# Pooling branch of a mixer: u computed in turned form, window sums by shifted adds on VectorE instead of band matrix products on TensorE

## What is computed

```python
proj = h @ w_in                      # h: 256 x 1024, w_in: 1024 x 2048
q, k, v, u = proj[..., :512], proj[..., 512:1024], proj[..., 1024:1536], proj[..., 1536:]
a = chunked_attention(q, k, v, ...)  # 8 heads of 64
# pooling, group g with window w in (2, 4, 8, 16):
win_sum = c[:, 1:] - c[:, start]     # trailing sum over at most w frames
outs.append(win_sum / count - uf)    # count = min(t + 1, w)
y = einsum('bsgc,gcd->bsgd', d, pool_w) * pool_scale
out = concatenate([a, y], -1) @ w_out
```

## Time and profile before

| | |
|---|---|
| time of 3 runs, median (lowest to highest) | 713.96 us (713.49 to 714.18) |
| the profiled execution: its own time, its span | 713.59 us, 711.8 us |
| TensorE busy | 701.5 us, 99% of the span |
| VectorE, ScalarE, GpSimd busy | 482.0, 378.8, 59.0 us |
| chain of work that ended last | 98% on TensorE |

### The profile page before, as it was taken

How to read it: one execution, slowest core, us unless ns; L and a number is a source line. 1 busy time by engine, 2 the same in 40 slices (tenths; PEclk the granted TensorE clock), 3 DMA queues, 4 the chain that set the end, 5 groups by cost and what they waited for, 6 DMA issues and landing times.

```text
span 711.8 us, 9748 instructions
## 1 busy us (share of the span) xinstructions
PE 701.5 (99%) x3734; PEld 596.0 (84%) x3734; DVE 482.0 (68%) x730; ACT 378.8 (53%) x517; POOL 59.0 (8%) x36
## 2 busy tenths in 40 slices
PE   8999999999999999999999999999999999999995
PEld 7888888888888688888888888888888888878884
DVE  5696777755476456777776855466763738898756
ACT  6764555444376555754445644477444534675450
POOL 1000000000000400000000000000005172131001
PEclk9999999999999999999999999999999999999999
DMA  8987555555345314655455566436574183443001
GB/s 306 356 329 279 192 206 188 178 186 210 136 181 232 120 52 156 243 197 201 185 177 185 199 215 232 177 126 229 186 253 148 40 316 121 175 161 135 1 1 59
DMA packets 21523, 129.33 MB, mean 182 GB/s; under 512 B 2456, under 2 KB 4400, under 8 KB 7280
## 3 DMA queue, kind: packets, MB, share of 16 engines
q1 hardware_dynamic: 19872, 126.72, 48.8%
q10 hardware_dynamic: 1344, 1.32, 0.6%
q0 software_dynamic: 272, 0.81, 0.3%
HBM read 127.79 MB, written 1.06 MB: 181 GB/s over the span
## 4 chain that ended last, share of the span: by engine, by line
PE 98%; DVE 1%; DMA 1%; issue 0%; ACT 0%; DVEq 0%; POOLq 0%
PE ps L421 23%; PE ps L386 16%; PE ps L388 16%; PE ps L387 16%; PE ps L427 12%; PE ps L406 3%; PE ps L410 2%; PE ps L633 1%; PE ps L564 1%; PE ps L982 1%; PE ps L804 1%; PE ps L440 1%; DMA sm<-in_sm 1%; PE ps L580 1%; PE ps L688 1%; PE ps L690 1%
## 5 line engine op out<-in xcount | busy, mean ns | idle before, releaser
L1495 DVE TENSOR_TENSOR wlo<-raw,whi 128x2048 fp32r<-128x2048 f32 x69 | 159.1, 2314 | 39.0 <-ACT whi L1056 38.8
L1056 ACT ACTIVATE whi<-raw 128x2048 fp32r<-128x2048 f32 x78 | 148.8, 1910 | 44.2 <-PE ps L388 42.0
L421 PE MATMUL ps<-xt,whi 128*128 128x512 f32 x704 | 168.4, 391 | 0.0
L421 PEld LDWEIGHTS ps<-xt,whi 128*128 128x128 f32 x704 | 129.4, 188 | 25.0
L386 PE MATMUL ps<-whi,xt 128*128 128x512 f32 (+1 forms) x304 | 121.8, 401 | 0.1
L388 PE MATMUL ps<-whi,xt 128*128 128x512 f32 (+1 forms) x304 | 117.0, 385 | 0.0
L387 PE MATMUL ps<-wlo,xt 128*128 128x512 f32 (+1 forms) x304 | 116.8, 384 | 0.0
L427 PEld LDWEIGHTS ps<-xt,wlo 128*128 128x128 f32 x704 | 90.3, 191 | 3.4
L427 PE MATMUL ps<-xt,wlo 128*128 128x256 f32 x704 | 91.3, 283 | 0.0
L1448 POOL TENSOR_TENSOR wlo<-raw,whi 128x2048 fp32r<-128x2048 f32 (+1 forms) x9 | 41.0, 4559 | 549.6 <-ACT whi L1056 549.6
L1100 ACT ACTIVATE work<-ps 128x512 f32<-128x512 f32 x44 | 26.2, 598 | 96.1 <-PE ps L421 91.2
(11 more groups left out here) (238 smaller groups left out, 740.2 us busy)
## 6 DMA issues: line engine op xcount, KB each, us to landing
raw<-in_gu SPq DMA_DIRECT2D x41, 1024.0 KB, 4.8
raw<-in_dn SPq DMA_DIRECT2D x22, 1024.0 KB, 4.7
raw<-in_win SPq DMA_DIRECT2D x8, 1024.0 KB, 4.8
raw<-in_fqk SPq DMA_DIRECT2D x8, 1024.0 KB, 4.8
raw<-in_wout SPq DMA_DIRECT2D x4, 1024.0 KB, 5.2
raw<-in_fg SPq DMA_DIRECT2D x4, 1024.0 KB, 4.8
raw<-in_fv SPq DMA_DIRECT2D x4, 1024.0 KB, 4.8
raw<-in_fo SPq DMA_DIRECT2D x4, 1024.0 KB, 4.7
```

Source lines behind the costliest of these rows:

```text
L421: return pe.matmul(ps[:, banks[u], :], wh[:, k * S + u * P:k * S + (u + 1) * P], x, start=k == 0, stop=k == KD - 1)
L1056: act.activation(whi[:, c % RING, 0:n], raw[:, c % RING, 0:n], ACT.Copy).then_inc(hi_ready, 1)
L1495: dve.tensor_tensor(wlo[:, c % RING, 0:n], raw[:, c % RING, 0:n], whi[:, c % RING, 0:n].bitcast(F32), ALU.subtract).then_inc(lo_ready, 1)
```

## The change

TensorE now computes u already turned (channels on the partitions, frames along the row): the weights are stationary, 128 columns at a time, and the 256 frames move. `u_step(step)` has four channel blocks of three products of 256 columns, 12 products in place of 6; two steps make one group, and the groups come in the order of windows 16, 8, 4, 2. The band matrices and the copies to `u_sb` are gone, and with them the 8 band products, their 2 copies to `d_t`, and 1,472 of the 4,096 columns of a parameter transfer.

In their place: `mixer_row` turns the frames' scale factors into a row (2 transposes on TensorE, one copy `row(1, 3, mix_row)` on ScalarE ahead of `hi(C_WIN+5+RING)`). VectorE multiplies each group of u by that row into a padded row `u_pad` (`pool_begin`), forms window sums by doubling (`doubled`: the row plus itself shifted by 1, 2, 4, 8), corrects the first 16 frames (`fewer`) and takes the mean minus the frame into `d_t` (`pool_end`). Every such step waits for the one ahead of it. That is 4 multiplications, 10 doublings, 4 corrections and 4 final steps, put into the head loop behind `probs_out`; the last group's stand ahead of `outputs_lo(0)`. Four small memsets clear the pads earlier. The `pool_w` products wait for all four groups (`pooled`). GpSimd's program is the same as before.

```diff
+            def mixer_row():
+                pe.wait_ge(rstd_ready, 2)
+                for t in range(NT):
+                    m = pe.transpose(ps[:, 3, t * P:(t + 1) * P], rstd[:, t:t + 1].broadcast_to([P, P]), ident)
+                m.then_inc(row_psum, 1)
...
-            def u_step(k):
-                wh, wl = take(C_WIN + 6 + k // HALF)
-                for t in range(NT):
-                    w = slice((k % HALF) * BANK, (k % HALF + 1) * BANK)
-                    m = three(ps[:, 2 + t, :], xth[:, k, t * P:(t + 1) * P], xtl[:, k, t * P:(t + 1) * P], wh[:, w], wl[:, w], k == 0, k == KD - 1)
+            def u_step(step):
+                p, k0 = step // 2, step % 2 * HALF
+                wh, wl = take(C_WIN + 6 + p // 2)
+                if p == 1 and k0 == 0:
+                    pe.wait_ge(row_ready, 2)
+                if p >= 2 and k0 == 0:
+                    pe.wait_ge(u_turned, 4 + p - 1)
+                for k in range(k0, k0 + HALF):
+                    w = slice(k * S + p % 2 * P, k * S + p % 2 * P + P)
+                    m = three(ps[:, 2 + p % 2, 0:S], wh[:, w], wl[:, w], xth[:, k, :], xtl[:, k, :], k == 0, k == KD - 1)
...
+            mixer_row()
             u_step(0)
             scores1(0)
             for h in range(H1):
...
-                    pe.wait_ge(par_landed, 16)
-                    pe.wait_ge(u_ready, 2)
-                    for g in range(4):
-                        o = ps[:, 2 + g // 2, (g % 2) * S:(g % 2) * S + S]
-                        pe.matmul(o, u_sb[:, 0, g * P:(g + 1) * P], band[:, g, 0:S], start=True, stop=False)
-                        m = pe.matmul(o[:, P:S], u_sb[:, 1, g * P:(g + 1) * P], band[:, g, S:S + P], start=False, stop=True)
...
+            pe.wait_ge(par_landed, 16)
+            pe.wait_ge(pooled, 4)
             for g in range(4):
-                pe.wait_ge(d_act if g // 2 else d_dve, 1)
...
+            row(1, 3, mix_row)
             hi(C_WIN + 5 + RING)
...
+            def pool_step(i):
+                i.then_inc(pool_order, 1)
+                n_pool[0] += 1
+                dve.wait_ge(pool_order, n_pool[0])
...
+            def doubled(p, j):
+                src = u_pad[p % 2] if j == 0 else sum_pad[(j - 1) % 2]
+                back = 1 << j
+                pool_step(dve.tensor_tensor(sum_pad[j % 2][:, PAD:PAD + S], src[:, PAD:PAD + S], src[:, PAD - back:PAD + S - back], ALU.add))
...
+            def pool_begin(p):
...
+                dve.tensor_tensor(u[:, PAD:PAD + S], ps[:, 2 + p % 2, 0:S], mix_row, ALU.mult).then_inc(u_turned, 1)
+                dve.wait_ge(u_turned, 4 + p + 1)
+                for j in range((4 - p) // 2):
+                    doubled(p, j)
...
+            def pool_end(p):
+                g = 3 - p
+                for j in range((4 - p) // 2, 4 - p):
+                    doubled(p, j)
+                total = sum_pad[(3 - p) % 2]
+                first = total[:, PAD:2 * PAD]
+                pool_step(dve.tensor_tensor(first, first, fewer[:, g, :], ALU.mult))
+                dve.scalar_tensor_tensor(out=d_t[:, g, :], in0=total[:, PAD:PAD + S], scalar=1.0 / WINDOWS[g], in1=u_pad[p % 2][:, PAD:PAD + S],
+                                         op0=ALU.mult, op1=ALU.subtract).then_inc(pooled, 1)
...
             for h in range(H1):
                 masked(0, h, lambda t: bias1[:, h, P:2 * P] if t == 0 else bias1[:, h, :], 4)
-                if h == H1 - 1:
-                    dve.wait_ge(chunk_used, C_WIN + 8)
-                    dve.tensor_scalar(u_sb[:, 1, :], ps[:, 3, :], rstd[:, 1:2], None, ALU.mult).then_inc(u_ready, 1)
                 if h >= 1:
                     probs_out(0, h - 1, 6 + (h - 1) % 2)
                 if h % 2 == 0 and h >= 2:
                     rinv_of(h // 2 - 1)
                 if h in (4, 6):
                     divided(h // 2 - 2)
+                if h % 2:
+                    pool_begin(h // 2)
+                elif h:
+                    pool_end(h // 2 - 1)
+            pool_end(3)
             outputs_lo(0)
             rinv_of(3)
-            dve.wait_ge(d_psum, 1)
-            dve.tensor_copy(d_t[:, 0:2, :].rearrange("p g s -> p (g s)"), ps[:, 2, :]).then_inc(d_dve, 1)
             probs_out(0, H1 - 1, 6 + (H1 - 1) % 2)
```

More of the change, by code:

```diff
@@ L95 @@
 CS_MASK, CS_MASKM, CS_N = 0, 256, 512
-PA_BIAS, PA_BAND, PA_PW, PA_N = 0, 2048, 2048 + 1536, 4096
+PA_BIAS, PA_FIX, PA_PW, PA_LOADED, PA_N = 0, 2048, 2048 + 64, 2048 + 64 + 512, 4096
+WINDOWS = (2, 4, 8, 16)
+PAD = max(WINDOWS)
 PB_UK, PB_UV, PB_CA, PB_SA, PB_CI, PB_SI, PB_KVG, PB_LOADED = 0, 768, 1792, 1856, 1920, 1952, 1984, 2112
@@ L172, in build @@
         k1t = view(work, 1024, 1024, "p (k s) -> p k s", k=4)
-        u_sb = view(work, 2048, 1024, "p (t c) -> p t c", t=NT)
+        u_pad = [view(work, 2048 + i * (PAD + S), PAD + S) for i in range(2)]
+        sum_pad = [view(work, 2048 + 2 * (PAD + S), PAD + S), view(work, 6912, PAD + S)]
+        mix_row = view(work, 6656, S)
         v1 = view(work, 3072, 1024, "p (t c) -> p t c", t=NT)
@@ L177, in build @@
         bias1 = view(par, PA_BIAS, 2048, "p (h k) -> p h k", h=H1)
-        band = view(par, PA_BAND, 1536, "p (g s) -> p g s", g=4)
+        fewer = view(par, PA_FIX, 64, "p (g s) -> p g s", g=4)
         pool_w = view(par, PA_PW, 512, "p (g d) -> p g d", g=4)
@@ L793, in _ @@
                     pe.wait_ge(f_order, 1)
-                    pe.wait_ge(row_ready, 3)
+                    pe.wait_ge(row_ready, 4)
                 if h >= 2:
@@ L1113, in ffn @@
                     hi(C_GU[f] + RING)
-                    row(f, ROW, ffn_row)
+                    row(2 * f, ROW, ffn_row)
                     load_table(ACT.Silu)
@@ L1235, in _ @@
                     hi(C_WIN + 6 + RING)
-                if h == 6:
-                    act.wait_ge(chunk_used, C_WIN + 8)
-                    act.activation(u_sb[:, 0, :], ps[:, 2, :], ACT.Copy, scale=rstd[:, 0:1]).then_inc(u_ready, 1)
                 if h % 2 == 0 and h >= 2:
@@ L1244, in _ @@
                     outputs_hi(0)
-            act.wait_ge(d_psum, 2)
-            act.activation(d_t[:, 2:4, :].rearrange("p g s -> p (g s)"), ps[:, 3, :], ACT.Copy).then_inc(d_act, 1)
             spread_rinv(3)
@@ L1273, in _ @@
                 if nb == 0:
-                    row(2, 7, rstd_row)
+                    row(3, 7, rstd_row)
                     act.wait_ge(f_psum, 1)
@@ L1568, in ffn @@
                     sum_halves(0, 1)
-                dve.wait_ge(row_ready, f + 1)
+                dve.wait_ge(row_ready, 2 * f + 1)
                 times_row(0, 0)
@@ L1660, in _ @@
             norm(1)
+            for pad in u_pad + sum_pad:
+                dve.memset(pad[:, 0:PAD], 0.0).then_inc(u_turned, 1)
+            dve.wait_ge(u_turned, 4)
             dve.wait_ge(rstd_ready, 2)
@@ L1755, in _ @@
                                          op0=ALU.mult, op1=ALU.mult).then_inc(x2_ready, 1)
-            dve.wait_ge(row_ready, 3)
+            dve.wait_ge(row_ready, 4)
             dve.wait_ge(f_psum, 1)
@@ L2099, in constants @@
     s = np.arange(S)
-    band = np.zeros((P, 4, S + P), np.float32)
-    for g, w in enumerate((2, 4, 8, 16)):
-        start = np.maximum(s + 1 - w, 0)
-        inside = (s[:, None] <= s[None, :]) & (s[:, None] >= start[None, :])
-        m = inside / (s + 1 - start)[None, :].astype(np.float32) - np.eye(S)
-        band[:, g, :S] = m[:P]
-        band[:, g, S:] = m[P:, P:]
+    fewer = np.array([[w / min(t + 1, w) for t in range(PAD)] for w in WINDOWS], np.float32).reshape(1, -1)
     def rope(dim):
@@ L2113, in rope @@
         return by_tile(np.concatenate([c, c], 1)), by_tile(np.concatenate([-sn, sn], 1))
-    return eye, cst, band.reshape(P, -1), rope(ROPE), rope(IROPE)
+    return eye, cst, fewer, rope(ROPE), rope(IROPE)
 def arrays_of(i):
@@ L2122, in arrays_of @@
     i = {k: np.asarray(v) for k, v in i.items()}
-    eye, cst, band, rope_a, rope_i = constants()
+    eye, cst, fewer, rope_a, rope_i = constants()
     def blocks(w, kn, cols):
@@ L2148, in arrays_of @@
         a[f"dn{n}"] = down(i[f"ffn{n + 1}_w_down"][0])
-    a["win"] = blocks(i["w_in"][0], HALF, BANK)
+    u_from = 3 * H1 * DH1
+    u_groups = i["w_in"][0][:, u_from:].reshape(D, 4, P)[:, ::-1]
+    a["win"] = np.concatenate([blocks(i["w_in"][0][:, :u_from], HALF, BANK), blocks(u_groups.reshape(D, 4 * P), KD, S)])
     a["wout"] = halves_first(i["w_out"][0])
@@ L2163, in arrays_of @@
     bias[0:64, :, P + 64:2 * P] = -BIG
-    a["par1"] = np.concatenate([bias.reshape(P, -1), band, i["pool_w"][0].transpose(1, 0, 2).reshape(P, -1)], axis=1)
+    a["par1"] = np.concatenate([bias.reshape(P, -1), rows(fewer), i["pool_w"][0].transpose(1, 0, 2).reshape(P, -1)], axis=1)
     fox = i["fox_w_in_2"]
```

21 lines of the change are left out of this document (13 added, 8 removed).

## The result

| | before | changed |
|---|---|---|
| median of 5 runs each (lowest to highest) | 714.05 us (713.49 to 715.23) | 722.09 us (721.47 to 722.79) |
| ratio, 95% interval | | 1.0109 (1.0099 to 1.0120) |
| the profiled execution: its own time, its span | 713.59, 711.8 us | 721.47, 719.6 us |
| TensorE busy | 701.5 us | 701.8 us |

What follows compares the result with a forecast made beforehand. The prediction took TensorE to bound the kernel (98% of the chain of waits). TensorE's own -2.0 us and stalls of 7.7 us made +5.7, for a forecast of 719.4 us, range 716.4 to 721.6.

Steps and rivals of the forecast that it cites:

- TensorE's own work: TensorE in the changed stretch: band products -2.62, two transposes +0.21, products of u +0.40, sum -2.0 us.
- point 5: At attention_out(0, 0): TensorE waits for outputs_lo(0), now behind the last group's VectorE steps; stall 1.81 us.
- VectorE's steps: Added to VectorE's head loop: 0.44 us per multiplication or doubling, 0.17 per correction, 0.37 per final step, 8.3 us altogether.
- The collision: Head loop: doublings with two SBUF inputs are held until GpSimd's 4.6 us subtractions end, 2.2 and 3.3 us.
- exactly to the other's end: Argument from the earlier trace, around 617 to 622 us: a held VectorE or GpSimd instruction waits until the other's ends.
- Stalls: TensorE's waits in the head loop: values1(0) 1.15, scores1(2) 0.64, scores1(3) 3.57 us.
- Point 4: Turn of head 7: masked(7) stands behind pool_end(2), so its exponentials come late; stall 0.51 us.
- its own range of +4.9 to +6.5: Whole walk with VectorE steps of 0.36 to 0.50 us in place of 0.44: 718.5 to 720.5 us.
- longer than my stall: Kernel's end: clock at half over 5 us after the last product's start, longer than the 3.57 us stall.
- the stated range: Time of the whole changed kernel: 716.4 to 721.6 us around the forecast 719.4.
- the clock falls as well: Rival, 8%: TensorE's clock halves around the 3.57 us stall, another +1.5 to +3 us, 720.9 to 722.3.

Runs made afterwards that it cites:

- TensorE's part alone: Changed kernel without VectorE's doublings, corrections and final steps, only the multiplication by the row of scales kept: 713.45 us, ratio 0.9992.
- one input from PSUM: Changed kernel with doublings, corrections and final steps reading their first input from PSUM instead of SBUF: 715.88 us, ratio 1.0017.
- one SBUF input: Changed kernel with each doubling, correction and final step replaced by a constant multiplication of a single input in SBUF: 720.73 us, ratio 1.0086.
- changed, second: The changed kernel, unchanged, run and profiled again: 722.39 us (4 executions), ratio 1.0114.
- stall filled: Changed kernel plus ten unused 128 by 128 products on TensorE ahead of the scores of heads 6 and 7: 720.80 us, ratio 1.0098.
- GpSimd copies: Changed kernel with GpSimd's two operations in this stretch copying their first operand instead of subtracting the second: 716.61 us (one run).
- GpSimd later: Changed kernel with GpSimd's two lo parts held until at_lo 1 and at_lo 2, away from the doublings: 716.03 us, ratio 1.0025.
- second alone later: Changed kernel with only GpSimd's second lo part held, until outputs_lo(1), the first left in place: 717.03 us, ratio 1.0041.
- one input strided: Changed kernel with VectorE's steps as constant multiplications of a single SBUF operand read at a stride of two elements: 721.92 us (one run).

## Why the prediction missed

**TensorE's own work**: forecast -2.0, measured -2.1. The 256-column products at 0.12 us with a weight load each were right. That TensorE would idle at `attention_out` once the band products no longer fill the wait is in point 5. That 1.3 us of the 2.1 are lost there even without any window sum was not foreseen: the run of TensorE's part alone was expected to gain the whole 2.0.

**VectorE's steps**: 0.44, 0.17 and 0.37 us forecast; the starts above lie 0.21 (correction to final step) and 0.34 (final step to `masked`, at 240.03) apart, a pair of doublings 0.89. Right.

**The collision**: right in place and in who waits. The longest record is 3.6 us, forecast 3.7. Each held doubling ends 0.28 us behind GpSimd, forecast 0.4: it ends 0.14 earlier than GpSimd's end and its own 0.42 would give. The rows had that already. The copy ends at 619.78, and 619.78 + 2.28 is 622.06, not 621.9, while the held L1495 ends at 621.89; "exactly to the other's end" was some 0.15 us too strict. Stalls, forecast against measured: `values1(0)` 1.15 and 0.81, `scores1(2)` 0.64 and 0.51, `scores1(3)` 3.57 and 3.33; together 5.36 against 4.65. Points 4 and 5: 0.51 + 1.81 = 2.32 forecast. With no hold and no fall ahead of `attention_out`, the run with one input from PSUM is at +0.45 with TensorE's -2.1 in it, so they cost some 2.6, of which the list of waits shows 0.43 and 1.53; the other 0.6 it does not itemise. Point 4 blamed the exponentials of head 7; the profile names `probs_out` (L1632) at that wait, though the two end within 0.1 us of each other. Sum at full clock: **+5.1** (31.05 less 25.91), forecast +5.7, inside its own range of +4.9 to +6.5.

**The clock**: here the step failed. The forecast left it out of the sum and gave it 8%, on the argument that after the last product of the kernel the clock was low only over 5 us later, "longer than my stall". That took one execution for a bound. In its trace the fall is inside this stretch, at about 709.8, 5.2 us after the last product ended at 704.57:

```profile
709.00:710.00 1.00, 0.00 (x0) 0.00 (x0) 0.37 (x1) 0.00 (x0) 0.00 (x0) 0.90 0.48 182
```

In the second profile of the same kernel that product ends at 705.23 and the clock falls at about 707.7, 2.5 us later, and over all 14 profiles this distance is 2.5 to 5.2 us. At `scores1(3)` it was 4.7 and 3.8 us from the start of the idle time (changed, both profiles) and 2.2 with one SBUF input, at `attention_out` 1.5 to 2.5; in most of these TensorE had resumed by then. In the profiles the longest stall (3.33 us) was followed by a fall both times it stood unfilled, and it cost 1.5 us; the stall at `attention_out` (1.52 to 1.95 us) was followed by another in one of two, at 1.6 us. Two such stalls, where the forecast's rival had one.

So: 5.1 + 1.5 = 6.7 us in the first profile, 8.2 in the second; 714.1 and these give 720.8 and 722.3. The first would still lie in the stated range; the second fall, or a late start, is what carries the time past 721.6, and how many of the executions had that fall is not known. By their mean clocks (0.995 three times, 0.992 or 0.993 six times) all nine had at least one fall and six had two, one of which may lie at the start, as in the first profile. The nine executions of the changed kernel lie between 720.99 and 723.07, and the measured medians differ by 8.0 and 7.2. The forecast's rival "the clock falls as well" (720.9 to 722.3) was the case that came; with distances of 2.5 to 5.2 us between idling and fall it would have deserved far more than 8%, but only one of them was on record then.

**The start** looked in the first profile like a loss of 1.1 us that nobody had forecast. Over 14 profiles it lies between 225.15 and 228.17, and the two of the changed kernel are 227.11 and 225.15, so it is no effect of the change; it is also why medians here resolve no better than some tenths. All of the wander arises ahead of 15 us: from the fifth group of L580 (L584 or L585 after the change) on, which starts anywhere between 11.39 and 14.45, it is 213.7 to 213.8 us to the first transposes in all 14. Before it, the products of 512 columns follow each other at 0.24 us at best (changed, second, and stall filled: 225.15 and 225.31) and at 0.43 throughout at worst (GpSimd copies: 228.17). In eight of the 14 the granted clock itself shows a fall there, also in the second profile of the kernel before, from 8.0 to 11.4 us behind a stall of 2.62 us: such falls were in this kernel ahead of any change. Where the products are as slow without one, the view says 1.00, and these runs do not show why.

**What stays open.** Why a stall of 1.53 us was followed by a fall in four profiles (GpSimd later, one input from PSUM, second alone later, changed for the second time) and not in two others (stall filled, GpSimd copies). Nor is it the length of the stall: at the same place 1.90 to 1.95 us were followed by no fall in three profiles (changed for the first time, one SBUF input, one input strided). Of the eight slower executions of GpSimd later only one was profiled; for the others the mean clock gives the number of falls, not their place.

## What to carry to other kernels

Before adding SBUF-only steps to VectorE, lay GpSimd's records beside the places where they would run: each one met holds the step for what remains of it (2.1 and 3.3 us here, of which 1.5 and 3.2 reached TensorE), and everything queued behind pays. Ask of work that is taken off the bounding engine whether it was filling a wait: of 2.1 us saved, 0.8 was left. And a stall of some microseconds on TensorE in the middle of a kernel is to be priced with the clock that may fall behind it, here 1.5 or 1.6 us each time it fell.

## What the runs showed of the hardware

- VectorE held by GpSimd: a 0.42 us instruction issued while one of 4.6 us runs ends 0.28 us behind it. From GpSimd's end to the end of the pair it is 0.74 us both times, and 0.73 behind a copy of 1.9. Two SBUF inputs are not needed, one at the faster pace (0.29 us) does; with the first input from PSUM nothing is held (0.39 to 0.43 us each).
- The clock may fall after TensorE has resumed: it resumed at 249.86 and the clock fell at about 251.3 in the changed kernel, 253.24 and about 253.5 with GpSimd later. In these two the idle time itself shows 1.00, and the low stretch lasts some 3.4 us. With one SBUF input it fell at 248.0, with TensorE idle until 248.72, and stayed at 0.50 until about 254.8, twice as long.
